# Two-block transformer step on one core: DVE sums in PSUM banks, squares gathered by the vector engine, and an earlier and re-ordered weight queue

## The reference

```
hx = rmsnorm(x, g) * (1 + scale) + shift        # sum of squares over 2048 features
q, k, v, g_att, u_pool, ... = split(hx @ w_in[l])
y = concat(att * silu(..), pool * silu(..), conv * silu(..))
x = x + gate * (y @ w_out[l])
```

## Time and profile before

| | |
|---|---|
| timed executions, median of 3 | 3355.52 us |
| profiled execution, own time | 3353.54 us |
| its span, first to last instruction | 3351.8 us |
| mean granted TensorE clock | 0.974 |
| TensorE matmul busy (PE) | 3164.1 us, 94% |
| GpSimd busy (POOL) | 1894.6 us, 57% |
| ScalarE (ACT), VectorE (DVE) busy | 1444.4 us, 1278.4 us |
| HBM read | 609.13 MB, 182 GB/s over the span |

### The profile page before, as it was taken

How to read it: one execution, slowest core, us unless ns; L and a number is a source line. 1 busy time by engine, 2 the same in 40 slices (tenths; PEclk the granted TensorE clock), 3 DMA queues, 4 the chain that set the end, 5 groups by cost and what they waited for, 6 DMA issues and landing times.

```text
span 3351.8 us, 64404 instructions
## 1 busy us (share of the span) xinstructions
PE 3164.1 (94%) x25962; PEld 2836.3 (85%) x25962; DVE 1278.4 (38%) x2057; ACT 1444.4 (43%) x2177; POOL 1894.6 (57%) x756
## 2 busy tenths in 40 slices
PE   6899999999899996999897999999989999999999
PEld 4788886777677995878787988899989999999999
DVE  2137402554102327048206676486332443333000
ACT  3222223566223431257434565575444555554333
POOL 1234543323233667445454655567876888887887
PEclk9999999999899997999898999999999999999999
DMA  9786222211542971223693766444543555554555
GB/s 389 302 344 278 100 94 82 76 63 51 201 164 112 367 285 63 100 101 114 239 352 118 259 245 215 185 143 147 184 156 138 188 188 175 187 180 170 189 188 188
DMA packets 85970, 613.35 MB, mean 183 GB/s; under 512 B 9536, under 2 KB 10816, under 8 KB 12736
## 3 DMA queue, kind: packets, MB, share of 16 engines
q1 hardware_dynamic: 84672, 606.02, 49.3%
q10 hardware_dynamic: 1152, 5.24, 0.4%
HBM read 609.13 MB, written 2.10 MB: 182 GB/s over the span
## 4 chain that ended last, share of the span: by engine, by line
issue 58%; POOL 40%; POOLq 1%; PE 0%; DVE 0%; DVEq 0%
POOL w_low L543 40%; POOLq L538 0%; POOLq L542 0%; POOLq L543 0%; PE bank L579 0%; PE bank L581 0%; PE bank L580 0%; DVE region L2332 0%; DVEq L2332 0%; POOLq L2343 0%
## 5 line engine op out<-in xcount | busy, mean ns | idle before, releaser
L543 POOL TENSOR_TENSOR w_low<-raw,w_high 128x1024 fp32r<-128x1024 f32 x752 | 1894.4, 2533 | 1450.8 <-ACT w_high L1102 1447.4
L579 PE MATMUL bank<-h_high,w_high 128*128 128x256 f32 (+1 forms) x4416 | 1415.3, 320 | 48.5 <-POOL w_low L543 47.1
L580 PE MATMUL bank<-h_low,w_high 128*128 128x256 f32 (+1 forms) x4416 | 1393.4, 316 | 0.0
L581 PE MATMUL bank<-h_high,w_low 128*128 128x256 f32 (+1 forms) x4416 | 1393.3, 316 | 0.0
L1102 ACT ACTIVATE w_high<-raw 128x1024 fp32r<-128x1024 f32 x752 | 786.5, 1054 | 1160.6 <-PE bank L581 691.3
L579 PEld LDWEIGHTS bank<-h_high,w_high 128*128 128x128 f32 x4416 | 848.0, 192 | 136.8 <-issue 44.2
L581 PEld LDWEIGHTS bank<-h_high,w_low 128*128 128x128 f32 x4416 | 847.4, 192 | 51.0
L580 PEld LDWEIGHTS bank<-h_low,w_high 128*128 128x128 f32 x4416 | 848.1, 192 | 49.8 <-issue 0.7
L1102 ACT ACTIVATE region<-bank 128x512 f32<-128x512 f32 (+3 forms) x353 | 163.8, 472 | 390.1 <-PE bank L581 309.3
L557 PE MATMUL bank<-region,vec_sb 128*32 128x128 f32 x6016 | 197.8, 283 | 39.0 <-DMA region<-in_w_mods 38.8
L557 PEld LDWEIGHTS bank<-region,vec_sb 128*32 128x32 f32 x6016 | 164.4, 114 | 73.0 <-DMA region<-in_w_mods 44.7
(11 more groups left out here) (227 smaller groups left out, 3419.2 us busy)
## 6 DMA issues: line engine op xcount, KB each, us to landing
region<-in_w_mods SPq DMA_DIRECT2D x188, 1024.0 KB, 8.0
raw<-in_w_in SPq DMA_DIRECT2D x172, 1024.0 KB, 4.9
raw<-in_w_up SPq DMA_DIRECT2D x88, 1024.0 KB, 4.9
raw<-in_w_out SPq DMA_DIRECT2D x48, 1024.0 KB, 5.5
raw<-in_w_down SPq DMA_DIRECT2D x48, 1024.0 KB, 4.8
raw<-in_w_abr SPq DMA_DIRECT2D x8, 1024.0 KB, 4.9
raw<-in_w_sbr SPq DMA_DIRECT2D x8, 1024.0 KB, 4.9
region<-in_xin SPq DMA_DIRECT2D x1, 4096.0 KB, 14.3
```

The lines of the kernel that those rows point to most:

```text
L543: nc.gpsimd.tensor_tensor(WL[s][:, part], RAW[s][:, part], WH[s][:, part], ALU.subtract) \
L579: nc.tensor.matmul(bank[:, 0:n], WH[slot][:, w], h, start=first and j == 0, stop=False)
L580: nc.tensor.matmul(bank[:, 0:n], WH[slot][:, w], l, start=False, stop=False)
L581: end = nc.tensor.matmul(bank[:, 0:n], WL[slot][:, w], h, start=False, stop=last and j == len(blocks) - 1)
```

## The change

1. `add_squares` is gone from TensorE. DVE gathers the squares: the first is copied to bank `AUX[0]`, the next 14 are added there, the last add writes to SBUF, and one matmul with ones follows. It is called in DVE's residual loop for the tile before (`square_before`), for all three norms.
2. `small(1)` keeps its running sums in PSUM: the four convolution sums in banks `AUX[0]` and `AUX[3]`, the four pooling sums in `AUX[1]` and `AUX[2]`. Two copies bring the convolution's back to SBUF. `small(0)` is as before.
3. On the SyncE queue of `w_in1` the first four modulation units are loaded once `w_out0` is evacuated, ahead of `two(2)`, and the wait for `n_hl` is gone there.
4. On that of `w_out1`: `two(0)`, `two(1)`, then q0 and q1 after head 3 (`at1_y` at 4; buffers now at 0, 4096, 2048, 6144), q2 and q3 after head 7. `with_mods` gets `after=2`, `asked=4`: units 4, 5, then q4, q5, unit 6, q6, q7, unit 7, and so on to unit 15, then q24 to q31.

```diff
-    BUF_OUT1 = r2(0, 2048, 4096, 6144)
+    BUF_OUT1 = r2(0, 4096, 2048, 6144)
...
-            def with_mods(turns, unit0, per, buffers, i0=0):
+            def with_mods(turns, unit0, per, buffers, after=0, asked=0):
                 slots = len(buffers)
-                with sp.Fori(0, turns) as i:
+                if asked:
+                    for t in range(4):
+                        for q in range(max(per * t, asked), per * (t + 1)):
+                            sp.wait_ge(sem("mod_mm"), unit0 + q - slots + 1)
+                            mod_load(buffers[q % slots], q % slots, unit0 + q)
+                        unit(0, t + 2 + after)
+                with sp.Fori(1 if asked else 0, turns) as i:
                     for t in range(4):
                         for m in range(per):
                             q = per * t + m
                             sp.wait_ge(sem("mod_mm"), unit0 + q - slots + 1 + 4 * per * i)
                             mod_load(buffers[q % slots], q % slots, 4 * per * i + (unit0 + q))
-                        unit(i, t + 2 + 4 * i0)
+                        unit(i, t + 2 + after)
...
                 if l == 1:
                     two(0)
                     two(1)
-                sp.wait_ge(sem("n_hl"), H_AT[f"in{l}"] + KT)
+                    evacuated(sp, T_OUT[0] + 16)
+                    for q in range(4):
+                        mod_load(BUF_IN1[q], q, M_IN1 + q)
+                else:
+                    sp.wait_ge(sem("n_hl"), H_AT["in0"] + KT)
                 two(2)
...
-                    with_mods(4, M_IN1, 2, BUF_IN1, 1)
+                    with_mods(4, M_IN1, 2, BUF_IN1, 4, 4)
...
                 two(0)
-                sp.wait_ge(sem(f"at{l}_y"), 8)
                 if l == 0:
+                    sp.wait_ge(sem("at0_y"), 8)
                     with_mods(3, M_OUT0, 1, BUF_OUT0)
                 else:
-                    with_mods(3, M_OUT1, 2, BUF_OUT1)
+                    two(1)
+                    for q in range(4):
+                        sp.wait_ge(sem("at1_y"), 4 + 4 * (q // 2))
+                        mod_load(BUF_OUT1[q], q, M_OUT1 + q)
+                    with_mods(3, M_OUT1, 2, BUF_OUT1, 2, 4)
...
-                        if end == 4 or s >= 2:
-                            add_squares(name, width, 4 * i + (s - 2), s % 2, end == 1 and s == 2, False)
-            for k in (14, 15):
-                add_squares(name, width, k, k % 2, False, k == 15)
+            pe.wait_ge(sem("n_sums"), N_AT[name])
+            nc.tensor.matmul(AUX[0][:, 0:width], ONES, NT_[:, 3, 0:width], start=True, stop=True) \
+                .then_inc(sem("n_squsd"), 1)
...
+        def add_square(name, n, i, s):
+            count = 16 * N_AT[name] + s + 1 + 4 * i
+            static = isinstance(i, int)
+            dve.wait_ge(sem("n_sq"), count)
+            sq, sums = NT_[:, s % 2, 0:n], AUX[0][:, 0:n]
+            if static and i == 0 and s == 0:
+                V.tensor_copy(sums, sq).then_inc(sem("n_squsd"), 1)
+                return
+            dve.wait_ge(sem("n_squsd"), count + 1)
+            if static and i == 3 and s == 3:
+                add(NT_[:, 3, 0:n], sums, sq).then_inc(sem("n_sums"), 1)
+            else:
+                add(sums, sums, sq).then_inc(sem("n_squsd"), 1)
...
+            in_banks = lambda n0, n1: [AUX[n][:, a:a + T] for n in (n0, n1) for a in (0, T)]
+            conv = in_banks(0, 3) if l else [y[:, 4 + c, :] for c in range(4)]
+            pools = in_banks(1, 2) if l else [y[:, g, :] for g in range(4)]
...
-                    acc = st(y[:, 4 + c, :])[:, :, a:b]
+                    acc = st(conv[c])[:, :, a:b]
```

More of the change, by code:

```diff
@@ L467, in stream @@
                     two(1)
-                sp.wait_ge(sem("n_hl"), H_AT[f"in{l}"] + KT)
+                    evacuated(sp, T_OUT[0] + 16)
[3 more added lines that the diff above has]
+                    sp.wait_ge(sem("n_hl"), H_AT["in0"] + KT)
                 two(2)
                 if l == 0:
-                    with_mods(3, M_IN0, 4, BUF_IN0, 1)
+                    with_mods(3, M_IN0, 4, BUF_IN0, 4)
                     start = 9
                 else:
-                    with_mods(4, M_IN1, 2, BUF_IN1, 1)
+                    with_mods(4, M_IN1, 2, BUF_IN1, 4, 4)
                     start = 11
@@ L498, in stream @@
                         mod_load(buffers[q % len(buffers)], q % len(buffers), 12 * per + unit0 + q)
-                    if t < 2:
+                    if t < 2 and l == 0:
                         unit(3, t + 2)
@@ L1711, in norm, with square_before @@
                     low(at_, j, [(lo(j), T_BANK["in1"][j % 4][:, lower], unit + j, col, hi(j))])
+        def add_square(name, n, i, s):
[11 more added lines that the diff above has]
+                add(sums, sums, sq).then_inc(sem("n_squsd"), 1)
+        def square_before(name, n, i, s):
+            if s:
+                add_square(name, n, i, s - 1)
+            elif not (isinstance(i, int) and i == 0):
+                add_square(name, n, i - 1, 3)
         def rope(l, h):
@@ L1735, in small @@
             wdw, bdw = VEC["w_dw"][0] + l * 124, VEC["b_dw"][0] + 4 * l
+            in_banks = lambda n0, n1: [AUX[n][:, a:a + T] for n in (n0, n1) for a in (0, T)]
+            conv = in_banks(0, 3) if l else [y[:, 4 + c, :] for c in range(4)]
+            pools = in_banks(1, 2) if l else [y[:, g, :] for g in range(4)]
             for c in range(4):
-                own.mark(V.tensor_scalar(y[:, 4 + c, :], uc[:, c, :], VE[:, wdw + 31 * c + 15:wdw + 31 * c + 16],
+                own.mark(V.tensor_scalar(conv[c], uc[:, c, :], VE[:, wdw + 31 * c + 15:wdw + 31 * c + 16],
                                          VE[:, bdw + c:bdw + c + 1], ALU.mult, ALU.add))
@@ L1750, in small @@
             own.wait()
+            if l:
+                for n in range(2):
+                    own.mark(V.tensor_copy(y[:, 4 + 2 * n:6 + 2 * n, :], AUX[3 * n][:, 0:T2].rearrange("p (c t) -> p c t", t=T)))
+                own.wait()
             dve.sem_inc(sem("cv_conv"), 1)
@@ L1755, in small @@
             for g in range(4):
-                own.mark(V.tensor_copy(y[:, g, :], up[:, g, :]))
+                own.mark(V.tensor_copy(pools[g], up[:, g, :]))
             for off in [o_ for h in range(8) for o_ in (-1 - h, h + 1)][:15]:
@@ L1760, in small @@
                     a, b = max(0, -off), min(T, T - off)
-                    acc = st(y[:, g, :])[:, :, a:b]
+                    acc = st(pools[g])[:, :, a:b]
                     own.wait(len(groups) - 1)
@@ L1767, in small @@
                 for s in range(S):
-                    own.mark(mul(st(y[:, g, :])[:, s, :], st(y[:, g, :])[:, s, :], rc[:, g, :]))
+                    own.mark(mul(st(pools[g])[:, s, :], st(pools[g])[:, s, :], rc[:, g, :]))
             own.wait()
-            sub(y[:, 0:4, :], y[:, 0:4, :], up).then_inc(sem("cv_pool"), 1)
+            for g in range(4):
+                last = sub(y[:, g, :], pools[g], up[:, g, :])
+            last.then_inc(sem("cv_pool"), 1)
             dve.wait_ge(sem("cv_sum"), l + 1)
@@ L1990, in residual @@
                         mod_add(AUX[1 + s // 2], 2 * i + (32 + s // 2))
+                square_before(("in1", "fin")[l], T2, i, s)
             for first, end, x0, name in ((0, 2, 8, "x_in"), (2, 4, -8, "x_in2")):
@@ L2000, in _ @@
                         residual(i, s, x0)
+            add_square(("in1", "fin")[l], T2, 3, 3)
             evacuated(dve, T_OUT[l] + 16)
@@ L2297, in _, with residual2 @@
         dve.wait_ge(sem("x_norm"), KT)
-        with dve.Fori(0, 4) as i:
+        def residual2(i, s):
+            n = 4 * i + s
+            dve.wait_ge(halves_done, 2 * U_OUT2 + 2 * n + 2)
+            V.scalar_tensor_tensor(tile(RES, n), L[s][:, 0:T], MODF[:, ds(3 * n + 3 * 128 + 2, 1)], tile(RES, n),
+                                   ALU.mult, ALU.add).then_inc(bank_free[s], 1)
+            square_before("b2", T, i, s)
+        for s in range(4):
+            residual2(0, s)
+        with dve.Fori(1, 4) as i:
             for s in range(4):
[L2300 to L2303, removed]
+                residual2(i, s)
+        add_square("b2", T, 3, 3)
         evacuated(dve, T_OUT2 + 16)
```

## The result

The changed kernel takes 3425.39 us (median of 4 runs, 3423.86 to 3427.5), the kernel before 3355.69 in the same series; the ratio is 1.0205, 95% interval 1.0188 to 1.0223. The forecast was 3426. The profiled execution of after has a span of 3422.1 us, 70.3 more than before's; the sum said 70.9.

A forecast was written before the change was run, and what follows sets the result against it. TensorE, holding a matmul for 94% of the span, was taken as the bound. Terms -34.4 - 11.6 - 5.1 - 7.2 + 129.2 = +70.9 us gave 3426 us; its own range 3408 to 3444, the 8-in-10 range 3394 to 3465.

The forecast's parts named there:

- squares in `w_out0`: In `w_out0`, thirteen products with ones at 0.95 us leave TensorE's path, tail +0.7 us: -11.6 us.
- `w_in1` queue: At the start of `w_in1`, early q0 to q3 remove a 3.96 us wait and half-rate units at tile 4: -7.2 us.
- sums in banks: In layer 2, PSUM sums let GpSimd work under DVE's taps, ending TensorE's 31.7 us wait and slow restart: -34.4 us.
- `w_out1` queue and squares: In `w_out1`, ten tile periods of 22.3 us instead of 9.16, with small savings from squares: +129.2 us.
- squares in `w_out2`: In `w_out2`, thirteen tiles each save 0.43 us without the product with ones, tail +0.5 us: -5.1 us.
- the rest of the sum: The part outside `w_out1`'s new period, put at 60.9 us; faster overall if that period is under 15.2 us.
- the ring: In `w_out1`, tiles 3 to 12 each wait for a chain from the predecessor's end: split, loads, modulation, products; 22.3 us.
- the landing term: In `w_out1`, weight unit and two modulation units take 10.6 us from first issue to last landing; bounds 7.3 to 12.
- The rival by which the ring does not close: In `w_out1`, loads of tile t go out before tile t-1 ends: sum -84 us, 3271 us; 4%.
- The rival by which PSUM sums lock GpSimd out as well: In layer 2, PSUM sums still keep GpSimd out, so the 34.4 us stay: 3461 us; 5%.
- The rival of a clock that stays at half: In `w_out1` tiles 3 to 12, products take 11.6 us, period 28.1, 58 us more: 3484 us; 9%.
- quicker landing: In `w_out1`, loads land in 7.6 us, period 19.3, 30 us less: 3396 us; 13%.

The follow-up runs named there:

- experiment 1: The changed kernel with only `w_out1`'s queue altered: modulation units of tile t again ahead of weight unit t+2, early four kept; 3275.66 us, ratio 0.9752 to the kernel before.
- experiment 2: The kernel before with only the changed kernel's `w_out1` queue and the places of its buffers; 3485.59 us, ratio 1.0378 to the kernel before.
- experiment 3: The changed kernel with `w_out1`'s modulation units of tile t behind weight unit t+2; 3313.89 us, ratio 0.987 to the kernel before.
- experiment 9: The changed kernel with the two modulation units issued ahead of weight unit t+3 in `w_out1`, not behind it; 3399.61 us, ratio 1.0133 to the kernel before.
- experiment 5: The changed kernel with layer 2's convolution and pooling sums in SBUF again, without the two copies back; 3458.81 us, ratio 1.0306 to the kernel before.
- experiment 8: The kernel before, sums in SBUF, with each layer 2 convolution tap waiting for the one before it to end; 3322.93 us, ratio 0.9901.
- experiment 10: The kernel before, sums in SBUF, with one layer 2 convolution tap in eight waiting for the one before it to end; 3327.2 us, ratio 0.9909.
- experiment 6: The changed kernel without the early modulation units in `w_in1`, the wait for `n_hl` back as well; 3430.06 us, ratio 1.0212 to the kernel before.
- experiment 7: experiment 1 with the squares summed by TensorE again in all three output projections; 3303.72 us, ratio 0.984 to the kernel before.
- experiment 4: The changed kernel with ten extra products of constants ahead of the modulation units of tiles 3 to 12 in `w_out1`; 3424.6 us, ratio 1.0209 to the kernel before.

## Why the prediction was right, point by point

I laid the two traces over each other matmul by matmul; a step's size is how far the lag of after against before moves across it. 1.7 us of the lag are there before the first changed instruction. The rows of `w_out0` and `w_out2` end at the first product behind the norm, that of `w_out1` at its last tile.

| step | predicted | in the traces |
|---|---|---|
| squares in `w_out0` | -11.6 | -7.6 |
| `w_in1` queue | -7.2 | -5.2 |
| sums in banks | -34.4 | -34.5 |
| `w_out1` queue and squares | +129.2 | +126.8 |
| squares in `w_out2` | -5.1 | -5.4 |
| elsewhere (start +1.7, between `w_out1` and `w_out2` -4.5, last stage -1.1) | 0 | -3.9 |
| sum | +70.9 | +70.2 |

The sum is nearer than its terms. The steps miss by 4.0, 2.0, -0.1, -2.4, -0.3 and -3.9 us, and these nearly cancel; that the total fits within 1 us is luck. What is not luck is the sign and the size of the one large term. Two slips in the recorded text changed nothing: the rest of the sum is 60.5 and not 60.9, and a landing 0.9 us sooner gives 3417; the lower end of 3408 needs one 1.8 us sooner.

- *`w_out1`.* Ten periods of 22.2 us were predicted as 22.3, and the two ends of the ring are as said. By the mean of the ten, the issue comes 3.5 us after the residual (3.7 predicted), the second unit begins 10.0 us behind that (10.6 to its landing), and 8.8 us later comes the residual (2.2 + 5.8 = 8.0). So the landing was taken 0.6 us too long, the second unit and the products together 0.8 too short, and that cancels. In the period shown the last part is 7.7 us, in the next 8.9, since its products take 7.05 instead of 6.0: the clock comes back only on the way (granted 0.66 from 1741 to 1744, 0.98 from 1719 to 1722). Tile 2 came 1.3 us sooner than taken. Experiments 1 and 2 show that this order is needed and enough, 3 that it goes by the distance, 9 the landing term. The rival by which the ring does not close is out for this change, but it was priced well: 3271 us, and with the ring opened (experiment 1) it is 3275.66. There the stretch gains 19.4 us against before, 9.6 of it up to tile 2 by the early units, where at most 14.4 were allowed, the rest by the squares.
- *Sums in banks.* -34.5, and 33.4 by experiment 5. The rival by which PSUM sums lock GpSimd out as well is out. But my reason, two operands in SBUF, was half of it. The Trainium skill ("SBUF — State Buffer", section "SBUF: two separate sides") says that the shared pair is held "for the whole instruction". By that GpSimd should get in after one tap of 0.47 us. The trace of before shows 46.7 us, so what counts there is the run; experiments 8 and 10 show that a break between two taps lets GpSimd in.
- *Squares.* This step was mis-sized, 11.6 for 7.6 us in `w_out0`; 0.6 of the difference lies between tiles 1 and 2, ahead of the first product saved, in a stretch that takes 27.7 to 29.3 us in the other executions. The period falls by 0.85 us, not by the 0.95 that lies between the two starts in the earlier trace rows. In every fourth step the product had been covering DVE's `mod_add`, for which TensorE now waits; those steps gain 0.2 to 0.6. And at the tail the one product left runs cold behind a wait for DVE's add, 2.08 us for what took 1.02 in the earlier trace rows, which makes the tail 1.6 us late, not 0.7. Behind the norm 1.1 of that come back, since the first products run at half rate for 3.5 us and not for 6.1; they stand in the row of `w_in1`.

```profile
958.94 1.08 PE L572 MATMUL bank<-region,vec_sb 128*32 128x128 f32 x32 [0.34 <-DVE mod_sb L1842]
...
1060.85 2.08 PE L699 MATMUL bank<-region,const_sb 128*128 128x512 f32 x2 [2.50 <-DVE region L1680]
```

- *`w_in1`.* Tile 4 comes 7.3 us sooner, as predicted (7.2). But I followed units 0 to 3 and took the order behind them as the old one. The earlier tile 4 means that tile 6's units, 4 and 5, are wanted as much earlier, and unit 5 was not there: 1.43 us of wait, a unit at half rate (the last row under experiment 6) and the first products behind it, at a granted clock of 0.50, give back 3.2. With the 1.1 us from above that is the -5.2 of the table.
- *Elsewhere.* The -4.5 us between the two stages are open. Experiments 1, 7 and 9 have -3.2, -1.7 and -3.0 there, so some of it is scatter; 1.3 us are shorter waits of TensorE for ScalarE.
- The rival of a clock that stays at half is out: the 48 products took 6.0 and 7.05 us in the two periods, not 11.6. That of a quicker landing is out by the period.

## What to carry to other kernels

When loads are issued early, count the new distance: in a single in-order queue, whatever stands behind a load that waits for a buffer inherits its wait, and if that wait is for work one tile back, the stage turns into a ring with the whole landing in it. Ask of each load whose end its predecessor in the queue waits for. A saving ahead of a seam moves the next need forward as well, so the order behind it has to be followed one or two tiles further than the change reaches.

## What the runs showed of the chip

- An unbroken run of 120 DVE taps with two SBUF operands (start to start 0.39 us) kept one GpSimd instruction out for 46.7 us. With one tap in eight waiting for its predecessor (some 0.12 us of break) none took over 3.05 us, and the tap it met took up to 2.66 us.
- The same taps with their sums in PSUM take no longer: 46.07 us for 120, 0.473 us each by the median, against 0.466.
- Of three loads of 1 MiB issued together those issued first land first: 4.9 us for the first, 7.8 by the median for the pair behind it; with the pair first it is 5.9 for the pair and 8.9 for the third.
- A single pair of instructions after a wait of 2.50 us ran at half rate (2.08 against 1.02 us). Some 8.8 us of filler work ahead of each landing (experiment 4) kept the second unit behind it at the full clock in three periods of ten.
